# Five products of the input projection moved into the embedding and the experts' sum

## Chip, cores and metric

The kernel runs on one core of one Trainium2 chip. The metric is the device time of one execution in microseconds, the median of several runs. The engines are TensorE (PE; PEld is its weight load), VectorE (DVE), ScalarE (ACT), GpSimd (POOL) and SyncE (SP), which issues the DMAs.

## Reference, cut to what matters

The model is a stack of two mixed blocks (attention, a bidirectional recurrence, experts) and a third block of another kind. Only the start of each of the two mixed blocks is touched:

```python
h = _layer_norm(jnp.concatenate([meta, x], axis=1), emb_ln_g, emb_ln_b)   # the embedding
for li in range(DEPTH):                                                   # DEPTH = 2
    proj = h @ w_in[li]                                                   # the input product
    c_q, c_kv, k_pe, rw = _split(proj, [Q_LORA, KV_LORA, QK_ROPE, RWKV_COLS])
    y_att = _mla(c_q, c_kv, k_pe, cos, sin, ...)      # begins with rms norms of c_q and c_kv
    u = _centred_shift(rw, rwkv_mu_prev[li], rwkv_mu_next[li])
    ...
    ff = _hier_moe(...)                                                   # the experts and their sum
    h = _layer_norm(DN_ALPHA * h + ff, ln2_g[li], ln2_b[li])
```

There are 1040 tokens (16 meta tokens and 1024 others) of 1024 features; `w_in[li]` has 2368 columns.

## The kernel before, in words

**Stages.** The program is a sequence of stages, each written out per engine; between two of them every engine waits with `over` (L291) for all counts of the stage before. The stages here are the embedding (`embed_*`, L457 to L541), the input product with the small products of the attention's start (the front, `front_*`, L684 to L1110), and, after the experts of layer 0, their sum (`combine_*`, L2544 to L2630), which ends in the h of layer 1. The front of layer 1 follows it.

**Precision.** A float32 operand is split into two halves of the type fp32r: ScalarE copies it into `hi` (rounded), VectorE or GpSimd writes `lo` = x - hi. A product is three matmuls for each of the 8 slices of 128 features (`three`, L274): hi·hi, hi·lo, lo·hi.

**Tiles of tokens.** The embedding and the sum go over NT = 10 tiles of C = 104 tokens in rounds (`aged`, L451): in round r one step is done for tile r, the next for tile r-1, and so on. In the embedding the rounds are: statistics of tile r (L311 to L314); affine step of tile r-1 (L323, L326, L328); for tile r-2 the copy of its transposes into `hT.hi` (ScalarE, L524) and the subtraction into `hT.lo` (VectorE, L510). TensorE transposes a tile as soon as its affine step is done, in two halves of four 128-column pieces (L287), into six banks of PSUM in turn (eight in the sum), and waits for the subtraction of the tile that had the bank. The sum has one stage more: for tile r ScalarE scales the row of h (L2588), then VectorE adds two experts' rows times their gates (L2606), then the same norm, copy (L2583) and subtraction (L2615). SP stores each tile's h (L482, L2568) and loads the tile four further on into the same buffer once its transposes and its store are over (L470, L2552, L2554).

**The front.** `COLS` lists 19 blocks of 128 columns of w_in: two of the queries' low rank (n = 0, 1), one of keys and values (2), one of 64 columns for the rotated keys (3), and 15 of the recurrence. `GROUPS` cuts the tokens into groups of 416, 416 and 208, that is tiles 0 to 3, 4 to 7, 8 and 9. `front_order` (L577) yields (n, g) block by block, and with each the small products that stand behind it: `sum q` behind (2,1), which needs the squares of both query blocks over all tokens; `scale q` from (3,0) on, `turn pe` (the rotation of the keys, first user of the angles) from (4,0) on. The result of (n, g) goes into bank (3n + g) mod 6 of PSUM, small results into banks 6 and 7.

Weights have three buffers, `w[n % 3]`. SP loads block n+3 after product (n, 2) (`project_load`, L661); ScalarE makes `hi` (L867) during the block before, in the order of its list; `lo` is made by VectorE for even n and GpSimd for odd n (`half_lo`, L758, subtraction in L761). The products of the queries, of keys and values and of the rotated keys are copied out by ScalarE (L892). The angles of the rotation are worked out by VectorE in eight parts (`positions_dve`, L387) spread over the first eight steps of the front of layer 0; ScalarE makes sine and cosine behind (1,2) (`positions_act`, L426); SP stores and reloads them from (2,2) on (`positions_store`, L366).

In layer 0 the loads of blocks 0 to 2 are issued behind tiles 1 to 3 of the embedding, in layer 1 in the list at the start of the sum (`project_first`, L672). All their halves are made after the stage is over.

## Time and profile before

| | us |
|---|---|
| median of 3 runs | 5400.27 (5394.4 to 5401.44) |
| the profiled execution | 5393.46 |
| its span in the profile | 5391.6 |

| engine | busy us, share of the span |
|---|---|
| PE | 4819.5, 89% |
| PEld | 4154.7, 77% |
| DVE | 3312.1, 61% |
| ACT | 2134.1, 40% |
| POOL | 1304.3, 24% |

All times in rows are microseconds from the first instruction unless marked ns. "Idle before" is how long the engine had stood still, and the name behind the arrow is what ended it. The granted clock is a share of 2.4 GHz. SPq is SP's queue: the duration of a DMA row is that of its issue, not of the transfer.

### The profile page before, as it was taken

How to read it: one execution, taken by the hardware profiler on the slowest of the kernel's cores; microseconds unless marked ns; L12 is line 12 of the kernel's file. 1: busy time of each engine (PE TensorE's matmuls, PEld its weight loads, DVE VectorE, ACT ScalarE, POOL GpSimd, SP SyncE). 2: the span in 40 equal slices, each digit the busy share in tenths (PEclk: the TensorE clock that was granted, in tenths of full speed). 3: DMA queues.
4: the chain of work that ended last, by engine and by line, in shares of the span. 5: the costliest groups of instructions: out<-in, count | busy, mean ns of one | idle time of the engine just before them, and what ended most of it. 6: DMA issues, size and time to landing. Idle time of an engine off the chain costs nothing. (4 is left out here: it accounts for less than half of the span.)

```text
span 5391.6 us, 128874 instructions
## 1 busy us (share of the span) xinstructions
PE 4819.5 (89%) x56564; PEld 4154.7 (77%) x56564; DVE 3312.1 (61%) x5055; ACT 2134.1 (40%) x3885; POOL 1304.3 (24%) x940
## 2 busy tenths in 40 slices
PE   6989999998799957989999997799957988999999
PEld 5888888886588847878888886588845766788887
DVE  5435665557788864345665557788875465662662
ACT  2323333332188842433333332188843244232331
POOL 0012333332144510012333332144411100122221
PEclk9999999998799977989999998799978989999999
DMA  4420101003366653410101004366652101233332
GB/s 135 140 53 19 32 20 31 19 19 114 119 229 254 251 174 97 124 53 20 31 20 31 19 19 115 120 231 251 251 172 86 39 1 67 90 98 121 110 98 106
DMA packets 383087, 536.31 MB, mean 99 GB/s; under 512 B 136483, under 2 KB 306595, under 8 KB 354467
## 3 DMA queue, kind: packets, MB, share of 16 engines
q1 hardware_dynamic: 339714, 488.61, 28.3%
q0 software_dynamic: 41472, 34.21, 2.1%
q8 instruction: 450, 7.37, 0.6%
q10 hardware_dynamic: 1344, 5.24, 0.3%
q14 instruction: 107, 0.87, 0.1%
HBM read 573.01 MB, written 122.09 MB: 129 GB/s over the span
## 5 line engine op out<-in xcount | busy, mean ns | idle before, releaser
L280 PE MATMUL ps<-w_hi,xbT 128*128 128x512 f32 x1536 | 502.3, 398 | 18.0 <-DVE w L2437 18.0
L280 PE MATMUL ps<-hT,w_in 128*128 128x416 f32 (+1 forms) x2736 | 490.7, 338 | 9.0 <-DVE w_in L761 9.0
L280 PEld LDWEIGHTS ps<-hT,w_in 128*128 128x128 f32 x2736 | 457.3, 195 | 35.3 <-issue 29.3
L2437 DVE TENSOR_TENSOR w<-w,w_hi 128x2048 fp32r<-128x2048 f32 x192 | 429.9, 2278 | 2.2 <-ACT w_hi L2394 2.2
L1486 POOL TENSOR_TENSOR lm<-Ab,consts 116x416 f32<-116x416 f32 x240 | 254.8, 1069 | 592.0 <-PE ps L280 316.4
L2394 ACT ACTIVATE w_hi<-w 128x2048 fp32r<-128x2048 f32 x192 | 359.0, 1935 | 0.0
L280 PEld LDWEIGHTS ps<-w_hi,xbT 128*128 128x128 f32 x1536 | 289.6, 189 | 86.3 <-DVE w L2437 27.1
L280 PE MATMUL ps<-w,xbT 128*128 128x512 f32 x768 | 300.6, 391 | 0.0
L280 PE MATMUL ps<-v,pT 104*104 104x128 f32 (+1 forms) x2176 | 270.3, 280 | 28.2 <-issue 27.4
L2468 DVE TENSOR_TENSOR w<-w,w_hi 128x2048 fp32r<-128x2048 f32 x96 | 223.5, 2328 | 97.0 <-ACT w_hi L2430 97.0
L280 PEld LDWEIGHTS ps<-v,pT 104*104 104x104 f32 (+1 forms) x2176 | 248.8, 178 | 39.9 <-issue 32.4
L280 PE MATMUL ps<-w_hi,actT 128*128 128x512 f32 x768 | 253.5, 391 | 5.0 <-DVE actT L2463 5.0
L280 PE MATMUL ps<-x1T,w_gate 128*128 128x512 f32 x1056 | 249.5, 392 | 2.9 <-DVE x1T L3279 1.6
L280 PE MATMUL ps<-x1T,w_up 128*128 128x512 f32 x1056 | 246.5, 389 | 0.0
L280 PE MATMUL ps<-w_down,act 128*128 128x512 f32 x1056 | 241.6, 391 | 3.0 <-POOL w_down L3505 3.0
L280 PE MATMUL ps<-w_out,mixT 128*104 128x512 f32 x960 | 237.2, 403 | 2.3 <-DVE mixT L2046 2.3
L280 PEld LDWEIGHTS ps<-x1T,w_gate 128*128 128x128 f32 x1056 | 200.0, 190 | 45.5 <-issue 1.9
L280 PEld LDWEIGHTS ps<-w_down,act 128*128 128x128 f32 x1056 | 199.3, 189 | 45.0 <-POOL w_down L3505 3.4
L280 PEld LDWEIGHTS ps<-x1T,w_up 128*128 128x128 f32 x1056 | 198.2, 188 | 41.1
L3496 POOL TENSOR_TENSOR w_up<-w_up,w_up 128x1024 fp32r<-128x1024 f32 x44 | 116.1, 2640 | 459.1 <-ACT w_up L3418 459.1
L280 PE MATMUL ps<-T,lm 52*52 52x52 f32 x6400 | 192.2, 209 | 27.9 <-DVE TT L1430 19.6
L280 PEld LDWEIGHTS ps<-w_out,mixT 128*104 128x104 f32 x960 | 160.3, 169 | 71.7 <-DVE mixT L2046 11.2
(449 smaller groups left out, 11384.9 us busy)
## 6 DMA issues: line engine op xcount, KB each, us to landing
w<-in_moe_w_dram SPq DMA_DIRECT2D x192, 1024.0 KB, 10.0
w_gate<-in_w_gate_dram SPq DMA_DIRECT2D x44, 512.0 KB, 3.9
w_up<-in_w_up_dram SPq DMA_DIRECT2D x44, 512.0 KB, 3.9
w_down<-in_w_down_dram SPq DMA_DIRECT2D x44, 512.0 KB, 3.2
w_in<-in_w_in_dram SPq DMA_DIRECT2D x36, 512.0 KB, 4.3
ys<-t_ys SPq DMA_DIRECT2D x20, 832.0 KB
t_h<-x SPq DMA_DIRECT2D x30, 416.0 KB
w_out<-in_w_out_dram SPq DMA_DIRECT2D x24, 512.0 KB, 7.3
```

The costliest lines, as they stand in the source:

```text
L280: made = e.matmul(out, a, b, start=start, stop=stop)
L1486: e.tensor_tensor(m.LM[lv % 2][0:HP], m.ab[0:HP, :, 0, :], bc(m.lmask[0:HP, H * lv:H * lv + H].unsqueeze(1), [HP, 8, H]), ALU.mult).then_i ...
L2394: e.activation(w.hi, w.x, ACT.Copy).then_inc(*P.c("moe_act").tick(li, "w13", b, k))
L2437: e.tensor_tensor(w.lo, w.x, w.hf, ALU.subtract).then_inc(*P.c("moe_dve").tick(li, "w13", b, k))
L2468: e.tensor_tensor(w.lo, w.x, w.hf, ALU.subtract).then_inc(*dv.tick(li, "w2", b))
L3496: e.tensor_tensor(w.lo, w.x, w.hf, ALU.subtract).then_inc(*po.tick(0, c, "lo", f))
```

## The change

Five products of each layer, (0,0), (1,0), (2,0), (0,1) and (1,1), are issued by the embedding (layer 0) and by the experts' sum of layer 0 (for layer 1). TensorE goes through their slices with one generator for the five; behind the transposes of the embedding's tiles 0 to 9 stand 0, 0, 0, 0, 5, 5, 5, 5, 4, 16 of the 40 slices, behind those of tiles 4, 5, 6, 8, 9 of the sum 8 each. A product of block 0 waits for the subtraction of the last tile of its token group. Transposes use banks 6 and 7 for even tiles, 2 and 5 for odd ones, and wait for the subtraction two tiles back. The halves of blocks 0 to 2 are made inside the tiles: `hi` by ScalarE in rounds 2 to 4, `lo` by GpSimd for all three. ScalarE copies the five results out in late rounds. In layer 0 SP issues the three weight loads before the tiles instead of behind tiles 1 to 3. The front goes over the rest in the same order; the squares, the angles' parts, the sine and cosine, their store and the first halves of block 3 get other places in it.

```diff
@@ embed_sp
     positions_sp(e, P)
+    for n in range(3):
+        project_load(e, P, 0, n)
     for t in aged(NT, 3):
...
-        if t[2] in (1, 2, 3):
-            project_load(e, P, 0, t[2] - 1)
     project_first(e, P, 0)
+def turn_bank(P, i, half):
+    return P.ps[((6, 7), (2, 5))[i % 2][half]]
@@ embed_act
-    for t in aged(NT, 3):
+    for r, t in enumerate(aged(NT, 3)):
...
+        front_early_act(e, P, 0, r, (7, 9, 10, 11, 11))
@@ embed_pe
+    products = front_early_pe(e, P, 0, P.c("emb_dve"))
...
-            if i >= 3:
-                e.wait_ge(*P.c("emb_dve").at(0, i - 3, "lo", half))
-            psv = columns(P.ps[b], C)
+            if i >= 2:
+                e.wait_ge(*P.c("emb_dve").at(0, i - 2, "lo", half))
+            psv = columns(turn_bank(P, i, half), C)
...
+        for _ in islice(products, (0, 0, 0, 0, 5, 5, 5, 5, 4, 16)[i]):
+            pass
+EARLY = [(0, 0), (1, 0), (2, 0), (0, 1), (1, 1)]
+def late_order(li):
+    for n, g, here in front_order(li):
+        if (n, g) in EARLY:
+            assert not here
+        else:
+            yield n, g, here
@@ front_sp
-        if (n, g) == (2, 2) and li == 0:
+        if (n, g) == (3, 1) and li == 0:
             angles()
+def lo_taker(P, n):
+    return P.c("prj_pool" if n % 2 or n < 3 else "prj_dve")
+def front_early_pool(e, P, li):
+    for n in range(3):
+        half_lo(e, P, li, n, lo_taker(P, n))
+def front_hi(e, P, li, n):
+    w = P.frt.w[n % 3]
+    e.wait_ge(*P.d(f"prj_w{n % 3}_in").at(li, n))
+    e.activation(w.hi, w.x, ACT.Copy).then_inc(*P.c("prj_act").tick(li, "hi", n))
+def front_early_act(e, P, li, r, rounds_out):
+    if 2 <= r < 5:
+        front_hi(e, P, li, r - 2)
+    for at, (n, g) in zip(rounds_out, EARLY):
+        if at == r:
+            front_low_rank(e, P, li, n, g)
+def front_product(e, P, li, n, g):
+    w, (t0, tn) = P.frt.w[n % 3], GROUPS[g]
+    out = P.ps[(3 * n + g) % 6][:, 0:tn]
+    if g == 0:
+        e.wait_ge(*lo_taker(P, n).at(li, "lo", n))
+    if n >= 2:
+        e.wait_ge(*P.c("prj_act").at(li, "out", n - 2, g))
+    for k in range(8):
+        made = mms(e, three(out, w.at(k), P.hT.at(k, slice(t0, t0 + tn)), k == 0, k == 7))
+        if k == 7:
+            made.then_inc(*P.c("prj_pe").tick(li, n, g))
+        yield k
+def front_early_pe(e, P, li, rests):
+    for n, g in EARLY:
+        if n == 0:
+            e.wait_ge(*rests.at(0, 4 * g + 3, "lo", 1))
+        yield from front_product(e, P, li, n, g)
@@ front_act
-    hi(0)
-    for n, g, here in front_order(li):
+    for n, g, here in late_order(li):
-        if g == 0 and n + 1 < len(COLS):
-            hi(n + 1)
+        if ((n, g) == (2, 2) or n >= 3 and g == 0) and n + 1 < len(COLS):
+            front_hi(e, P, li, n + 1)
+        if (n, g) == (1, 2):
+            square(0, P.cq[:, 0, :], prj.at(li, "out", 0, 2))
+        if (n, g) == (2, 1):
+            square(1, P.cq[:, 1, :], prj.at(li, "out", 1, 2))
...
-        if (n, g) == (1, 2) and li == 0:
+        if (n, g) == (2, 2) and li == 0:
             positions_act(e, P)
@@ front_dve
-    half_lo(e, P, li, 0, prj)
+    angles = {(0, 2): (0, 1), (1, 2): (2, 3), (2, 1): (4, 5), (3, 0): (6, 7)}
...
-        if li == 0 and n < 3 and 3 * n + g < 8:
-            positions_dve(e, P, 3 * n + g)
+        for part in angles.get((n, g), ()) if li == 0 else ():
+            positions_dve(e, P, part)
@@ combine_act
+        if li == 0:
+            front_early_act(e, P, 1, r, (7, 8, 9, 11, 12))
@@ combine_pe
+    products = front_early_pe(e, P, 1, P.c("com_dve")) if li == 0 else None
...
+        if li == 0 and i in (4, 5, 6, 8, 9):
+            for _ in islice(products, 8):
+                pass
@@ gpsimd_program
+    front_early_pool(e, P, 0)
     for li in range(DEPTH):
...
+        if li == 0:
+            front_early_pool(e, P, 1)
```

## Rows read from the trace of the kernel before

**Rows 1.** Busy time by stretch: PE, PEld, DVE, ACT, POOL, clock, DMA, GB/s
```profile
340.00:360.00 20.00, 20.00 (x138) 19.55 (x135) 7.80 (x8) 5.02 (x7) 0.00 (x0) 1.00 0.00 1
```

**Rows 2.** Timeline of PE in the fronts: start, us, instructions, [idle before]
```profile
69.47 34.59 PE L280 MATMUL ps<-hT,w_in 128*128 128x416 f32 x192 [4.49 <-DVE w_in L761]
103.89 3.74 PE L280 MATMUL ps<-consts,squares 128*104 128x1 f32 x40
107.49 9.07 PE L280 MATMUL ps<-hT,w_in 128*128 128x208 f32 x48
...
2103.47 9.09 PE L280 MATMUL ps<-hT,w_in 128*128 128x208 f32 x48
```

**Rows 3.** Timeline of the embedding, layer 0: transposes and a tile's statistics
```profile
28.25 1.65 PE L287 MATMUL ps<-consts,x 104*128 104x104 f32 x8 [3.33 <-DVE x L328]
29.11 0.68 DVE L311 BATCH_NORM_STATS2 stat<-x 104x6 f32<-104x512 f32 x1
...
63.33 1.65 PE L287 MATMUL ps<-consts,x 104*128 104x104 f32 x8 [1.94 <-DVE x L328]
```

**Rows 4.** Timeline of the experts' sum, layer 0: the split of tile 7, the last transposes
```profile
2054.89 1.09 DVE L2615 TENSOR_TENSOR hT<-ps,hT 128x416 fp32r<-128x416 f32 x2 [0.77 <-ACT hT L2583]
...
2058.62 1.65 PE L287 MATMUL ps<-consts,h 104*128 104x104 f32 x8 [6.88 <-DVE h L328]
```

**Rows 5.** Timeline of ACT in the front of layer 0: copies of products
```profile
76.11 0.52 ACT L892 ACTIVATE cq<-ps 128x416 f32<-128x416 f32 x1 [7.10 <-PE ps L280]
80.64 0.52 ACT L892 ACTIVATE cq<-ps 128x416 f32<-128x416 f32 x1 [4.01 <-PE ps L280]
83.30 0.34 ACT L892 ACTIVATE cq<-ps 128x208 f32<-128x208 f32 x1 [2.15 <-PE ps L280]
...
112.07 0.35 ACT L892 ACTIVATE ckv<-ps 128x208 f32<-128x208 f32 x1 [4.13 <-PE ps L280]
```

**Rows 6.** Busy time by stretch, with the granted clock (columns as in rows 1)
```profile
70.00:75.00 5.00, 5.00 (x20) 4.82 (x19) 4.91 (x11) 0.00 (x0) 1.54 (x1) 1.00 0.68 204
104.00:112.00 8.00, 8.00 (x66) 8.00 (x65) 0.22 (x1) 2.07 (x3) 0.00 (x0) 0.79 0.01 2
...
2040.00:2060.00 20.00, 4.67 (x24) 3.99 (x24) 17.72 (x25) 4.36 (x10) 0.00 (x0) 0.50 0.23 65
...
2066.00:2068.00 2.00, 2.00 (x7) 1.91 (x6) 0.94 (x6) 0.00 (x0) 0.85 (x1) 0.50 1.02 227
...
2070.00:2072.00 2.00, 2.00 (x11) 1.98 (x11) 0.00 (x0) 0.00 (x0) 0.00 (x0) 0.92 1.05 364
```

**Rows 7.** View of the tile w_in: durations in ns (min/median/max), landing
```profile
L761 POOL TENSOR_TENSOR w_in<-w_in,w_in x18: 2363/2418/3166, 69.2 to 2346.8; 128x1024 fp32r<-128x1024 f32 x18
...
DMA to landing us min/median/max: 3.3/4.2/30.4
```

**Rows 8.** Timelines of POOL and of DVE in the front, near 194 us
```profile
194.71 2.42 POOL L761 TENSOR_TENSOR w_in<-w_in,w_in 128x1024 fp32r<-128x1024 f32 x1 [29.95 <-ACT w_in L867]
...
194.82 2.75 DVE L1078 TENSOR_TENSOR staged<-staged,cos 128x416 f32<-128x416 f32 x1
```

**Rows 9.** Timeline of DVE in the front of layer 0: first use of the angles
```profile
139.98 0.58 DVE L1076 TENSOR_TENSOR turned<-ps,sin 64x416 f32<-64x416 f32 x1 [0.41 <-PE ps L280]
```

**Rows 10.** Timeline of SP: a tile's load, weights in layer 1, the cosines
```profile
23.67 0.31 SPq L470 DMA_DIRECT2D x<-in_x_dram  x1
...
112.48 0.59 SPq L369 DMA_DIRECT2D t_cossin<-cos  x1
...
1962.61 27.57 SPq L669 DMA_DIRECT2D w_in<-in_w_in_dram  x3
```

**Rows 11.** Waits of DVE in the embedding, then in the sum: us, times, longest
```profile
DVE stat L311 <- DMA x<-in_x_dram: 1.4, 3, 0.7
...
DVE h L2606 <- ACT h L2588: 3.5, 1, 3.5
```

**Rows 12.** DMA issues up to 75 us: KB each, us to landing
```profile
rest<-in_positions_dram SPq DMA_DIRECT2D x1, 256.0 KB, 15.6
```

More of the change, by code:

```diff
@@ L2 @@
 from contextlib import ExitStack
-from itertools import groupby
+from itertools import groupby, islice
 import numpy as np
@@ L484, in embed_sp @@
             load(t[2] + 4)
-        if t[2] in (1, 2, 3):
-            project_load(e, P, 0, t[2] - 1)
     project_first(e, P, 0)
+def turn_bank(P, i, half):
+    return P.ps[((6, 7), (2, 5))[i % 2][half]]
 def embed_part(P, i, half):
-    return P.emb.hT.at(slice(4 * half, 4 * half + 4), slice(C * i, C * i + C)), columns(P.ps[2 * (i % 3) + half], C)
+    return P.emb.hT.at(slice(4 * half, 4 * half + 4), slice(C * i, C * i + C)), columns(turn_bank(P, i, half), C)
 def embed_dve(e, P):
@@ L761, in half_lo, with front_low_rank @@
     e.tensor_tensor(w.lo, w.x, w.hf, ALU.subtract).then_inc(*count.tick(li, "lo", n))
+def lo_taker(P, n):
[7 more added lines that the diff above has]
+    e.activation(w.hi, w.x, ACT.Copy).then_inc(*P.c("prj_act").tick(li, "hi", n))
+def front_low_rank(e, P, li, n, g):
+    kind, j, _, wd = COLS[n]
+    t0, tn = GROUPS[g]
+    into = P.cq[:, j, :] if kind == "q" else P.ckv if kind == "kv" else P.kpe
+    e.wait_ge(*P.c("prj_pe").at(li, n, g))
+    e.activation(into[0:wd, t0:t0 + tn], P.ps[(3 * n + g) % 6][0:wd, 0:tn], ACT.Copy).then_inc(
+        *P.c("prj_act").tick(li, "out", n, g))
+def front_early_act(e, P, li, r, rounds_out):
[21 more added lines that the diff above has]
+        yield from front_product(e, P, li, n, g)
 def front_pool(e, P, li):
-    for n in range(1, len(COLS), 2):
-        half_lo(e, P, li, n, P.c("prj_pool"))
+    for n in range(3, len(COLS), 2):
+        half_lo(e, P, li, n, lo_taker(P, n))
 def small_bank(number):
@@ L793, in spread @@
                  True) for k in range(tn // C) for to, x in parts]
-    for n, g, here in front_order(li):
-        w, (t0, tn) = m.w[n % 3], GROUPS[g]
-        if g == 0:
-            e.wait_ge(*P.c("prj_pool" if n % 2 else "prj_dve").at(li, "lo", n))
-        if n >= 2:
-            e.wait_ge(*P.c("prj_act").at(li, "out", n - 2, g))
-        out = P.ps[(3 * n + g) % 6][:, 0:tn]
-        mms(e, [y for k in range(8) for y in three(out, w.at(k), P.hT.at(k, slice(t0, t0 + tn)), k == 0, k == 7)]
-            ).then_inc(*prj.tick(li, n, g))
+    for n, g, here in late_order(li):
+        for _ in front_product(e, P, li, n, g):
+            pass
         for number, name in here:
@@ L872, in square @@
         e.activation(m.sums[k], src, ACT.Square).then_inc(*ac.tick(li, "square", k))
-    hi(0)
     earlier = []
-    for n, g, here in front_order(li):
+    for n, g, here in late_order(li):
         kind, j, _, wd = COLS[n]
         t0, tn = GROUPS[g]
-        if g == 0 and n + 1 < len(COLS):
-            hi(n + 1)
-        src = P.ps[(3 * n + g) % 6]
-        if kind == "u":
+        if ((n, g) == (2, 2) or n >= 3 and g == 0) and n + 1 < len(COLS):
[4 more added lines that the diff above has]
+            square(1, P.cq[:, 1, :], prj.at(li, "out", 1, 2))
+        if kind != "u":
+            front_low_rank(e, P, li, n, g)
+        else:
+            src = P.ps[(3 * n + g) % 6]
             dst, src = m.pt[n % 2][:, 1 + t0:1 + t0 + tn], src[:, 0:tn]
@@ L887, in front_act @@
                 e.wait_ge(*dv.at(li, "right", 1))
-        else:
-            into = P.cq[:, j, :] if kind == "q" else P.ckv if kind == "kv" else P.kpe
-            dst, src = into[0:wd, t0:t0 + tn], src[0:wd, 0:tn]
-        e.wait_ge(*P.c("prj_pe").at(li, n, g))
-        e.activation(dst, src, ACT.Copy).then_inc(*prj.tick(li, "out", n, g))
+            e.wait_ge(*P.c("prj_pe").at(li, n, g))
+            e.activation(dst, src, ACT.Copy).then_inc(*prj.tick(li, "out", n, g))
         if kind == "u" and g == 2:
@@ L1001, in front_dve @@
     earlier, turned = [], None
[L1002 to L1003 removed]
+    angles = {(0, 2): (0, 1), (1, 2): (2, 3), (2, 1): (4, 5), (3, 0): (6, 7)}
+    for n, g, here in late_order(li):
+        if n >= 3 and g == 0 and n + 1 < len(COLS) and (n + 1) % 2 == 0:
             half_lo(e, P, li, n + 1, prj)
[L1005 removed]
+        if n >= 3 and g < 2:
             shifted(n - 1, g)
[L1007 to L1008 removed]
+        for part in angles.get((n, g), ()) if li == 0 else ():
+            positions_dve(e, P, part)
         if (n, g) == (3, 0):
@@ L2540, in combine_part @@
     s = (P.xT2 if li else P.hT).at(slice(4 * half, 4 * half + 4), slice(c0, c0 + C - skip))
-    return s, columns(P.ps[2 * (i % 4) + half], C)[:, :, skip:C]
+    return s, columns(turn_bank(P, i, half), C)[:, :, skip:C]
 def combine_sp(e, P, li):
@@ L2574, in combine_act @@
     m, ac = P.com, P.c("com_act")
-    for t in aged(NT, 4):
+    for r, t in enumerate(aged(NT, 4)):
         if t[1] is not None:
```

22 lines of the change are left out of this document (5 added, 17 removed).

## The prediction

> **What bounds the kernel now.** The page puts TensorE first, so I went to its rows by stage. Inside the input product it never rests: it is busy in all of 340 to 360 us [rows 1], and from 69.47 us its rows follow each other without a gap [rows 2]. Any matmul taken out there is time taken off, as long as nothing else arrives late. In the two stages ahead of it, the embedding and the experts' sum of layer 0 (called the sum below), VectorE sets the pace and TensorE waits: in a tile's round it transposes for 1.65 us and sits idle for 3.33 us, in the sum 6.88 us [rows 3, 4]. So the change moves matmuls from a stage that TensorE bounds into two that it doesn't. I write (n,g) for the product of block n with token group g.
>
> **Price of a product.** The copies of (0,0), (0,1) and (0,2) start at 76.11, 80.64 and 83.30 us [rows 5]: 4.53 us for 24 matmuls of 416 columns, 2.66 us for 24 of 208. The five early ones are all of 416: 22.65 us a layer.
>
> **Layer 0, the path.** Before: the last transposes end at 63.33 + 1.65 = 64.98 us [rows 3]; then TensorE idles 4.5 us until block 0 is split; product (0,0) to (2,1) run to 103.89, the 40 matmuls of the sum of squares to 107.49, (2,2) to 111.9 (its copy starts at 112.07) [rows 2, 5]. That is 46.9 us from the last transpose to the start of (3,0). After: (0,0), (1,0) and (2,0) are over by then. Their 24 steps of three matmuls go 5, 5, 5, 5, 4 behind tiles 4 to 8; 15 matmuls take 15/24 of 4.53 = 2.83 us, and with the transposes' 1.65 us this is 4.5 us in a round of some 5.0, so the next transposes aren't late by more than 0.3 us. Behind tile 9 come (0,1) and (1,1), 9.06 us, of which only the former 4.5 us of idling is cover; then (0,2) and (1,2) 5.32, (2,1) 4.53, sum of squares 3.60, (2,2) 4.4. Sum 26.9, with the 0.3 us 27.2 us. **Gain 46.9 - 27.2 = 19.7 us.** It is less than 22.65 + 4.5, since two of the five "early" products stand behind the last tile in the path, and more than three products since the split of block 0 and the slow start go.
>
> **The clock.** (2,2) costs 4.4 us and not 2.66 us since it runs after the one-column matmuls: 104 to 112 us has a granted clock of 0.79, a mix of 1.2 and 2.4 GHz [rows 6]. The change keeps that order, so I keep the price. The sum runs at 0.50 (1.2 GHz). The front of layer 1 begins after 4.5 us of idling like that of layer 0, at 2064.8 us, and still has 0.50 in 2066 to 2068 and 0.92 in 2070 to 2072 [rows 6]. I take 5.5 us at the slow level: 15.8 matmuls of 416/1.2 = 347 ns, then 8.2 of 189 ns, 7.05 us for a first product. In layer 0 the stretch 70 to 75 us reads 1.00 but holds only 20 matmuls, 250 ns each [rows 6]; I take it as the same rise. The first steps behind tile 4 then take 5.2 us and push the transposes of tile 5 by 1.4 us; ScalarE copies those only a round later, so nothing waits. The Trainium skill, "TensorE: Matmul & The Clock Gate" (Part 1), says that the slow level is the resting state and that sustained work releases it; the rows of the sum agree.
>
> **Layer 1, the path.** Before: the transposes end at 2058.62 + 1.65 = 2060.27 us [rows 4], and (3,0) starts 4.4 us after the row of 2103.47 us [rows 2], at 2107.9: 47.6 us. After: (0,0) waits behind the transposes of tile 4 for the split of tile 3, in the next round; (0,0), (1,0) and (2,0) then fit into rounds that leave TensorE 6.88 us each. (0,1), behind the transposes of tile 8, waits for the split of tile 7: 2054.89 + 1.09 = 2056.0 us [rows 4], with TensorE at the slow level again. It takes 7.05 us, to 2063.0, so the transposes of tile 9 end at 2064.65 instead of 2060.27. From there (1,1) 4.53, (0,2) and (1,2) 5.32, (2,1) 4.53, 3.60, 4.4: (3,0) starts at 2087.0 instead of 2107.9. **Gain 20.9 us.**
>
> **What the change adds.** Three splits a layer go to GpSimd, 2.42 us each [rows 7], and three first halves to ScalarE, inside the tiles. ScalarE is mostly idle there. GpSimd is another matter. At 194.82 us a VectorE multiply with two SBUF inputs lasts 2.75 us because a split on GpSimd began 0.11 us ahead of it [rows 8]; free, an operation of that width takes 0.58 us [rows 9]. VectorE is the bound of the tiles' stages. In the embedding GpSimd's split falls due while VectorE is in its last affine step, and behind it stand the transposes' subtraction (one input in PSUM) and the statistics (one input), 1.08 + 1.5 us, which hide 2.4 us: 0. In the sum, the two products with the gates stand right behind the affine step, both with SBUF inputs. Block 0's load was issued at 1962.6 and the longest landing is 30.4 us [rows 7, 10]: it lands about 1992.5, and ScalarE, which waits for it in order, gives the square root and the copy of tile 0 some 2.7 us late. That delay and GpSimd's splits of blocks 0 and 1 (2.3 us) come ahead of a wait of VectorE of 3.5 us for tile 4's row [rows 11], which swallows most of it: left 1.6 us, then the split of block 2, 2.3 us. I take 3.9 us; bounds 0 and 3 x 2.4 = 7.2 us.
>
> **Loads of layer 0.** The three weight loads (1.5 MB) now stand ahead of the first store of h. The queue had drained by 4.5 + 15.6 = 20.1 us [rows 12]; now it drains about 5 us later. Tile 4's load waits for that store: issued at 23.67 before [rows 10], some 4 us later now, so it lands near 32 us and the statistics of 29.11 us [rows 3] start 2.8 us late. In return the three waits of VectorE on later tiles, 1.4 us [rows 11], go, since no weights compete there. Net loss 1.4 us; bounds: a gain of 1.4 and a loss of 5.
>
> **Moved steps that I cost at nothing.** Block 3's load is issued after (0,2), at 77 us, behind SP's list of small loads; it lands 4.2 us later at the median [rows 7], its first half stands in ScalarE's queue behind the square root at 88 us, and the split ends at 91.8 us, just ahead of 92.2. The cover is (2,2) at the slow level; were (2,2) at 2.66 us, (3,0) would wait 1.4 us. In layer 1 SP's list comes 4.7 us later and block 3 is still ready before (3,0). The angles move behind (2,2): between the store of the cosines at 112.48 us [rows 10] and their first use at 139.98 us [rows 9] lie 27.5 us; now the store comes 8 us after the start of (3,0), at 100, and the use 28.1 us after it, at 120. The 20 us left cover a store, a reload and their issue at 4.2 us a landing. VectorE reaches the scaling of the queries later, and the next small product waits 0.7 us in layer 0: counted. The banks: transposes keep four instead of six or eight, but wait for a subtraction two tiles back, long done. The low-rank copies fall into idle time of ScalarE.
>
> **Sum.** Layer 0: 19.7 - 1.4 - 0.7 = 17.6. Layer 1: 20.9 - 3.9 = 17.0. Together 34.6 us. The profiled execution took 5393.46 us (span 5391.6) and would take 5358.9; it stands 6.8 us below the median of the runs, 5400.27, and from that the forecast is **5365.7 us**.
>
> **Rivals.** *(A) No losses.* The tiles' load comes in time, GpSimd finds gaps: 19.7 + 1.4 - 0.7 + 20.9 = 41.3 us, 5359 us. For it: a split that meets VectorE at a step with one input costs nothing. Chance 0.2.
> *(B) Each of the six splits holds VectorE in full*, 14.4 us instead of 3.9: gain 24.1, 5376 us. It needs VectorE at a two-input instruction each time. The Trainium skill, "SBUF — State Buffer" (Who interferes with whom), states this rule: whoever issues first gets the shared pair for the whole instruction, the other blocks; the rows at 194.8 us agree, and by it the time depends on what stands next in VectorE's queue. Chance 0.13.
> *(C) TensorE stays at 1.2 GHz through the tiles.* The 15 matmuls take 5.2 us, a round of the embedding 6.9 instead of 5.0: 9.5 us over five rounds, (0,1) and (1,1) 7.7 us more, in the sum some 5 us. Gain 12, 5388 us. Against it: at 2064.8 us the clock rose within 6 us of dense matmuls. Were the loads late as well, no change is left. Chance 0.05.
> *(D) Slower: the tiles starve.* Load of tile i waits for the store of tile i-4, and this queues behind weights. If each of the six later tiles came late, VectorE would pay each time; it decides from 7.6 us a tile (45.4 us lost against 34.6 gained): 5411 us. Against it: the queue is empty of weights after the first, and those waits were 0.7 us at most. Chance 0.02.
> That it doesn't do what it says is half true in layer 0 (two of five are behind the last tile) and in the sum already.
>
> **Chances.** Forecast 0.6. The range 5352 to 5381 us takes in (A), (B), the bounds above and a median that moves by a few us. A measurement here can tell 0.2%, 10.8 us, from no change: faster by more than that 0.94, within it 0.04, slower 0.02.
>
> **What would show it.** Right: matmuls of w_in from some 41 us on and from 2022 us on; (3,0) starting 92 to 95 us and near 2091 us; no idle time of TensorE there above 2 us. GpSimd's first three splits beside VectorE's two-input steps of some 3.5 us in the sum. Wrong: TensorE idle ahead of (3,0), rounds of the embedding above 5.5 us from tile 5 on, or a front stage that gives the time back after (3,0).

## The result and the profile after

The changed kernel takes 5363.57 us at the median of four runs (5362.61 to 5367.15), the kernel before 5399.22 us in four runs (5394.4 to 5401.44) made beside them: a ratio of 0.9933, 95% interval 0.9917 to 0.9949, that is 35.7 us less. The forecast was 5365.7 us. The profiled execution has a span of 5362.6 us, 29.0 us less than the 5391.6 of before; where the other 6 us of the profile stayed is told below.

The timeline of TensorE in the embedding and in the front of layer 0, changed kernel (columns: start, us, then engine, line, instruction, count, idle time before and what ended it):

```profile
40.92 1.65 PE L287 MATMUL ps<-consts,x 104*128 104x104 f32 x8 [3.33 <-DVE x L328]
42.27 4.04 PE L280 MATMUL ps<-hT,w_in 128*128 128x416 f32 x15
...
46.80 3.07 PE L280 MATMUL ps<-hT,w_in 128*128 128x416 f32 x15
50.88 0.93 PE L287 MATMUL ps<-consts,x 104*128 104x104 f32 x8 [1.01 <-DVE x L328]
...
64.43 0.93 PE L287 MATMUL ps<-consts,x 104*128 104x104 f32 x8 [0.37 <-DVE x L328]
65.14 19.19 PE L280 MATMUL ps<-hT,w_in 128*128 128x416 f32 x120
84.16 3.74 PE L280 MATMUL ps<-consts,squares 128*104 128x1 f32 x40
87.77 9.07 PE L280 MATMUL ps<-hT,w_in 128*128 128x208 f32 x48
96.67 1.93 PE L280 MATMUL ps<-consts,rms 104*128 104x104 f32 x16
```

The first rows answer to the embedding's of before [rows 3]: behind the transposes of tiles 4 to 7 now stand 15 matmuls each, and the idle time of 3.33 us ahead of the next tile's has shrunk to 1.2 at most. After the last tile TensorE doesn't stop; before it stood still for 4.49 us [rows 2]. The last row serves as a mark from here on: the first "spread" of the norm's factors, 16 matmuls right behind (3,0). Before it stood here:

```profile
116.40 1.93 PE L280 MATMUL ps<-consts,rms 104*128 104x104 f32 x16
```

So layer 0 is 19.73 us ahead at this mark. Some of that is scatter at the very start: the statistics of tile 1 begin at 15.15 us before and at 15.81 here, and counted from them it is 20.4 us. The same view for layer 1, from the sum to the same mark:

```profile
2007.56 6.11 PE L280 MATMUL ps<-hT,w_in 128*128 128x416 f32 x24 [4.29 <-DVE hT L2681]
...
2014.16 4.77 PE L280 MATMUL ps<-hT,w_in 128*128 128x416 f32 x24
...
2041.65 6.12 PE L280 MATMUL ps<-hT,w_in 128*128 128x416 f32 x24 [4.29 <-DVE hT L2681]
2047.61 0.88 PE L287 MATMUL ps<-consts,h 104*128 104x104 f32 x8
2048.26 14.66 PE L280 MATMUL ps<-hT,w_in 128*128 128x416 f32 x96
2062.76 4.90 PE L280 MATMUL ps<-consts,squares 128*104 128x1 f32 x40
```

The spread of layer 1 starts at 2076.89 us, 35.51 us ahead of the 2112.40 of before. The sum itself began 19.07 us earlier; SP's first load of it, before and after, is the second mark:

```profile
1957.98 0.33 SPq L2552 DMA_DIRECT2D ys<-t_ys  x1
```

```profile
1938.91 0.33 SPq L2616 DMA_DIRECT2D ys<-t_ys  x1
```

Layer 1 adds 16.44 us. What VectorE did in the sum's first rounds (timeline of VectorE, changed kernel; L323 and L328 are the affine steps, L2672 the products with the gates, L2681 the subtraction out of PSUM), and GpSimd beside it:

```profile
1976.18 1.09 DVE L2681 TENSOR_TENSOR hT<-ps,hT 128x416 fp32r<-128x416 f32 x2 [3.54 <-ACT hT L2647]
1977.18 1.98 DVE L323 SCALAR_TENSOR_TENSOR h<-h,stat,gain 104x1024 f32<-104x1024 f32 x1
...
1979.27 3.17 DVE L328 SCALAR_TENSOR_TENSOR h<-h,stat,bias 104x1024 f32<-104x1024 f32 x1
1982.37 2.59 DVE L2672 SCALAR_TENSOR_TENSOR h<-ys,gates,h 104x1024 f32<-104x1024 f32 x2
...
1990.88 4.69 DVE L2672 SCALAR_TENSOR_TENSOR h<-ys,gates,h 104x1024 f32<-104x1024 f32 x2
```

```profile
1975.73 2.35 POOL L781 TENSOR_TENSOR w_in<-w_in,w_in 128x1024 fp32r<-128x1024 f32 x1 [38.22 <-ACT w_in L796]
1978.52 2.84 POOL L781 TENSOR_TENSOR w_in<-w_in,w_in 128x1024 fp32r<-128x1024 f32 x1 [0.44 <-ACT w_in L796]
1990.28 2.89 POOL L781 TENSOR_TENSOR w_in<-w_in,w_in 128x1024 fp32r<-128x1024 f32 x1 [8.92 <-ACT w_in L796]
```

The affine steps lasted 1.27 and 1.28 us before, and take 1.98 and 3.17 where a split of GpSimd (the subtraction that makes `lo`) runs; the products with the gates of tile 4 lasted 2.61 and take 4.69: 0.71 + 1.89 + 2.08 us.

### The profile page after: what moved, and what is told of

It reads as the page before. It is cut to its first block and busy times, and to the rows that moved or that the text cites. A ratio compares the mean times of both kernels' runs of the same rounds, so it can differ in the third digit from the quotient of the medians.

```text
span 5362.6 us, 128881 instructions
## 1 busy us (share of the span) xinstructions
PE 4821.6 (90%) x56564; PEld 4156.3 (78%) x56564; DVE 3307.6 (62%) x5051; ACT 2133.3 (40%) x3885; POOL 1314.0 (25%) x944
## 5 line engine op out<-in xcount | busy, mean ns | idle before, releaser
L280 PEld LDWEIGHTS ps<-w_hi,xbT 128*128 128x128 f32 x1536 | 291.1, 190 | 87.0 <-DVE w L2501 27.2
```

Source lines behind the costliest of these rows:

```text
L280: made = e.matmul(out, a, b, start=start, stop=stop)
```

## The experiments

Each kernel was timed in rounds with the kernel before, and the ratio is against the median of the kernel before in the same rounds (5397.59 to 5402.88 us; 5399.22 is that of the first measurement). Since one median moves by a few us, I also read the marks in each profile: the first spread of layer 0, the start of the sum, the first spread of layer 1 and the span. What stands behind the third mark is the same program in all of them; the last column is the span less that mark. Where two numbers stand for "changed", the second is the second measurement (e5). The marks scatter too: the statistics of tile 1 start at 14.5 to 16.0 us, with every placing of the loads alike, and VectorE's first affine step of the sum, which waits for the row of the affine parameters, starts 18.3 to 20.2 us after the sum.

| kernel | median us | ratio (95%) | spread, layer 0 | sum starts | spread, layer 1 | sum to spread | span | rest |
|---|---|---|---|---|---|---|---|---|
| before | 5399.22 | | 116.40 | 1957.98 | 2112.40 | 154.42 | 5391.6 | 3279.2 |
| changed | 5363.57 / 5359.80 | 0.9933 / 0.9928 | 96.67 / 96.29 | 1938.91 / 1937.61 | 2076.89 / 2075.46 | 137.98 / 137.85 | 5362.6 / 5358.0 | 3285.7 / 3282.5 |
| e1 layer 0 alone | 5375.25 | 0.9959 (0.9946 to 0.9973) | 98.44 | 1937.22 | 2091.80 | 154.58 | 5377.6 | 3285.8 |
| e2 layer 1 alone | 5373.82 | 0.9954 (0.9940 to 0.9968) | 117.52 | 1961.67 | 2100.20 | 138.53 | 5375.8 | 3275.6 |
| e3 none inside | 5397.38 | 0.9998 (0.9989 to 1.0008) | 112.78 | 1954.68 | 2106.64 | 151.96 | 5392.2 | 3285.6 |
| e4 splits held | 5358.27 | 0.9923 (0.9909 to 0.9936) | 95.91 | 1933.92 | 2067.47 | 133.55 | 5357.4 | 3289.9 |
| e6 loads behind tiles | 5363.95 | 0.9942 (0.9929 to 0.9954) | 100.38 | 1943.17 | 2080.69 | 137.52 | 5359.9 | 3279.2 |
| e7 more slices | 5361.77 | 0.9931 (0.9918 to 0.9945) | 95.65 | 1938.62 | 2076.45 | 137.83 | 5358.6 | 3282.2 |
| e8 sums spread | 5361.88 | 0.9936 (0.9924 to 0.9949) | 98.09 | 1939.80 | 2077.83 | 138.03 | 5360.0 | 3282.2 |
| e9 loads, splits timed | 5362.69 | 0.9930 (0.9916 to 0.9943) | 98.28 | 1937.15 | 2068.25 | 131.10 | 5353.6 | 3285.3 |
| e10 all together | 5354.35 | 0.9918 (0.9904 to 0.9931) | 95.98 | 1934.70 | 2068.62 | 133.92 | 5347.8 | 3279.2 |
| e11 held, more slices | 5358.84 | 0.9920 (0.9907 to 0.9934) | 93.33 | 1934.77 | 2068.66 | 133.89 | 5358.2 | 3289.5 |
| e12 and loads behind tiles | 5358.40 | 0.9925 (0.9911 to 0.9938) | 93.00 | 1935.88 | 2068.79 | 132.91 | 5354.9 | 3286.1 |

### One layer alone

e1 keeps the sum, the front of layer 1 and GpSimd's program of before; e2 the embedding and the front of layer 0:

```diff
+def front_pe(e, P, li):                       # likewise sp, act, dve, pool
+    return (front_pe_whole if li == 1 else front_pe_rest)(e, P, li)   # e2: li == 0
-        if li == 0:                           # e1; combine_* as before
-            front_early_pool(e, P, 1)
-    front_early_pool(e, P, 0)                 # e2; embed_* as before
```

> The change in the embedding and the front of layer 0 alone; the sum of layer 0 and the front of layer 1 as before. Theory (the two halves are independent and nearly equal, 17.6 and 17.0 us by the prediction): gain 17.6 us against before, a ratio of 0.9967, and (3,0) of layer 0 starts near 92.2 us, (3,0) of layer 1 at 2107.9 - 17.6 = 2090 us. Rival (one half carries nearly all of the 35.7 us measured, the other gives its part back later): ratio at 0.993 or at 1.000.

> The change in the sum of layer 0 and the front of layer 1 alone; the embedding and the front of layer 0 as before. Theory: gain 17.0 us, ratio 0.9969; (3,0) of layer 1 starts near 2091 us; GpSimd's splits again hold VectorE in the sum (multiplies of 1.3 us at 2 to 3 us). Rival: as for the other half.

By the marks layer 0 alone is 17.96 us ahead at its spread, and its layer 1 takes the 154.6 us of before. Layer 1 alone takes 138.5 us from the start of the sum to the spread, 15.9 less than before, with the same stretched steps of VectorE. So in the marks the halves are independent and nearly equal, as the theory has it. The medians say 22.6 and 24.0 us. The interval of e1 takes in the expected ratio of 0.9967; that of e2 ends at 0.9968, just short of 0.9969. Both can't be right beside the 35.7 of the whole; the marks add up to 33.9. e2's profile also has the shortest rest of all, 3275.6 us, with the same instructions there: medians of five runs are too coarse to split a gain of this size.

### No product inside

```diff
-        for _ in islice(products, (0, 0, 0, 0, 5, 5, 5, 5, 4, 16)[i]):
+        for _ in islice(products, (0, 0, 0, 0, 0, 0, 0, 0, 0, 40)[i]):
...
-        if li == 0 and i in (4, 5, 6, 8, 9):
-            for _ in islice(products, 8):
+        if li == 0 and i == 9:
+            for _ in products:
```

ScalarE's copies of the five results move to the last round (round 11 for all five in the embedding, round 12 in the sum).

> Everything of the change but the place of the five products: in both layers all 40 slices stand behind the transposes of the last tile, and ScalarE copies the results out in its last round. Banks, halves and loads stay as changed. Theory (the gain is TensorE's idle time filled, the rest is small): layer 0 loses 24 slices x 0.566 us = 13.6 us of its gain; in layer 1 three products (13.6 us) and the one behind tile 8 (6.1 us at the slow clock, of which the transposes' own wait gave back some 4.4) come back, some 16 to 18 us. Together 30 to 32 us lost of 35.7: 4 to 6 us faster than before, ratio 0.999. Rival (the halves made early and the filled wait of 4.5 us ahead of the front are the main gain): ratio 0.996 or lower.

The median is 0.5 us below that of before, no difference; the marks give 3.62 us in layer 0 and 2.46 from the start of the sum to the spread, and at the last mark the kernel is 5.8 us ahead, in the range expected, of which its rest gave 6.4 back. TensorE, behind the last transposes of each layer:

```profile
65.11 33.71 PE L280 MATMUL ps<-hT,w_in 128*128 128x416 f32 x192
...
2059.47 34.82 PE L280 MATMUL ps<-hT,w_in 128*128 128x416 f32 x192
```

The idle time of 4.5 us between stage and front has gone here too, in both layers. That part of the change is real but small; the place of the matmuls carries the gain.

### GpSimd's splits in the sum

```diff
 def front_early_pool(e, P, li):
     for n in range(3):
+        if li:
+            e.wait_ge(*P.c("com_dve").at(0, 3 + n, "y", 1))
         half_lo(e, P, li, n, lo_taker(P, n))
```

> The changed kernel, but in the sum GpSimd starts each of its three splits only when VectorE has finished the products with the gates of tiles 3, 4 and 5, that is while VectorE stands at the statistics, a wait and the subtraction out of PSUM. Theory (the splits hold VectorE at instructions with two SBUF inputs: 0.7 + 1.9 + 2.1 us in the changed kernel's sum; the late weights' 2.8 us are swallowed by the wait for tile 4): the multiplies are back at 1.3 and 2.6 us, tile 4's statistics start 3.9 us earlier against the start of the sum, and the kernel is 3.9 us faster than the changed one (5359.7 us). Rival (the late weights alone set the time of tile 4): multiplies faster, tile 4's statistics where they were, same time as the changed kernel. Second rival (the splits hit other steps instead): three stretched instructions elsewhere, same time or slower.

The same rounds of VectorE, and GpSimd beside them:

```profile
1970.71 1.28 DVE L323 SCALAR_TENSOR_TENSOR h<-h,stat,gain 104x1024 f32<-104x1024 f32 x1
...
1972.09 1.28 DVE L328 SCALAR_TENSOR_TENSOR h<-h,stat,bias 104x1024 f32<-104x1024 f32 x1
...
1982.68 2.61 DVE L2674 SCALAR_TENSOR_TENSOR h<-ys,gates,h 104x1024 f32<-104x1024 f32 x2 [0.79 <-ACT h L2654]
```

```profile
1976.16 2.34 POOL L781 TENSOR_TENSOR w_in<-w_in,w_in 128x1024 fp32r<-128x1024 f32 x1 [43.62 <-DVE h L2674]
```

All three stretched steps are back at 1.28 and 2.6 us, and GpSimd's own are shorter (2.34 instead of 2.84 and 2.89). Tile 4's statistics start 51.41 us after the sum's first load, 56.70 in the changed kernel: 5.3 us earlier, where 3.9 were expected (0.9 us of the difference is the row of the affine parameters, which landed that much earlier against the sum's start); from the sum to the spread it is 4.43 us less. The cause of VectorE's loss is shown: the same instructions, the same loads, only the moment of the splits moved. The same holds for the four kernels below that hold these splits (e9 to e12): none of their affine steps and products with gates in the sum lasts over 1.31 us. The wait for tile 4 of 3.5 us [rows 11] is now one of 0.79: the late weights, which hold ScalarE back by 2.1 us here, took most of the rest, and tile 4's row came 0.6 us earlier. The median is 5.3 us below the first measurement of the changed kernel and 1.5 below the second; the medians alone would not carry the verdict.

### The changed kernel once more

> The changed kernel once more, unaltered, to see what one profile and another of the same program differ by. Theory (stretches with the same instructions differ between profiles by single steps of 1.6 to 2.9 us, where TensorE comes back from an idle stretch at 1.2 instead of 2.4 GHz, whatever the kernel): median within 3 us of 5363.6, the front of layer 0 ends its sum of squares and (2,2) within 2 us of the first profile, and the stretch behind the first small products of layer 1, 3285.8 us before, differs by several us. Rival (the 6.5 us that the profile gave back there belong to the change): that stretch is again within 1 us of 3285.8.

The rest behind the spread of layer 1 took 3282.5 us, 3.2 less than in the first profile of the same program, and in the other profiles of this unchanged stretch 3275.6 to 3289.9. The rival falls. The median, 5359.80 us, is 3.8 us from the first one's 5363.57, where at most 3 was expected. One such step: the experts of layer 1, where TensorE comes back after 2.7 us of idling. First the profile of the changed kernel above, then this one (PE's timeline, then busy time by stretch, in the columns of [rows 1]):

```profile
3489.03 0.79 PE L280 MATMUL ps<-w_hi,xbT 128*128 128x512 f32 x1 [2.72 <-DVE w L2501]
...
3490.00:3492.00 2.00, 2.00 (x6) 1.56 (x5) 2.00 (x2) 2.00 (x2) 1.85 (x1) 0.50 0.03 0
```

```profile
3481.16 0.50 PE L280 MATMUL ps<-w_hi,xbT 128*128 128x512 f32 x1 [2.73 <-DVE w L2501]
...
3482.00:3484.00 2.00, 2.00 (x10) 1.65 (x9) 2.00 (x2) 2.00 (x2) 1.73 (x1) 1.00 0.06 8
```

The same instructions after the same idle time, once at 1.2 GHz (granted clock 0.50, 6 matmuls in 2 us), once at 2.4 (10 matmuls). The profile of before had 1.00 here as well. This step costs 2.9 us by the time TensorE is back at 2.4 GHz; with one of 2.6 us in the output product ahead of it that is 5.5 of the 6.5 us that the first profile of the changed kernel gave back behind the mark; smaller ones of both signs stand beside them. What decides between the two levels these profiles don't show.

### The loads of layer 0

```diff
-    for n in range(3):
-        project_load(e, P, 0, n)
     for t in aged(NT, 3):
...
+        if t[2] in (1, 2, 3):
+            project_load(e, P, 0, t[2] - 1)
@@ front_early_act: halves of layer 0 in rounds 4 to 6
-    if 2 <= r < 5:
-        front_hi(e, P, li, r - 2)
+    at = 2 if li else 4
+    if at <= r < at + 3:
+        front_hi(e, P, li, r - at)
```

> The changed kernel with layer 0's weight loads back behind tiles 1 to 3 and the first halves of layer 0 made in rounds 4 to 6 instead of 2 to 4. Theory (the three loads ahead of the first store make tile 4's row 2.7 us late, and take away three small waits of 1.4 us): statistics of tile 4 at 29.1 instead of 31.8 us, waits of 0.4 to 0.7 us ahead of three later tiles, (3,0) of layer 0 1.4 us earlier, at 90.8 us. Rival (the delay of tile 4 is the queue's, full of the positions' small packets, and not the weights'): tile 4 as late as in the changed kernel, and the later waits on top: 1.4 us slower.

Tile 4 in the changed kernel, SP and VectorE, and then tile 4 here:

```profile
5.76 15.33 SPq L689 DMA_DIRECT2D w_in<-in_w_in_dram  x2
...
27.78 0.31 SPq L470 DMA_DIRECT2D x<-in_x_dram  x1
...
31.82 0.69 DVE L311 BATCH_NORM_STATS2 stat<-x 104x6 f32<-104x512 f32 x1 [1.69 <-DMA x<-in_x_dram]
```

```profile
28.88 0.69 DVE L311 BATCH_NORM_STATS2 stat<-x 104x6 f32<-104x512 f32 x1
```

Tile 4 is in time again, 2.9 us earlier, of which 0.9 is the earlier start of this profile (2.0 us counted from the statistics of tile 1): the first half of the theory holds. But the kernel is 3.7 us behind at the spread instead of 1.4 ahead. The splits now fall elsewhere:

```profile
37.51 3.17 DVE L328 SCALAR_TENSOR_TENSOR x<-x,stat,bias 104x1024 f32<-104x1024 f32 x1
...
43.04 3.05 DVE L323 SCALAR_TENSOR_TENSOR x<-x,stat,gain 104x1024 f32<-104x1024 f32 x1
...
51.17 3.18 DVE L328 SCALAR_TENSOR_TENSOR x<-x,stat,bias 104x1024 f32<-104x1024 f32 x1
```

```profile
37.22 2.38 POOL L781 TENSOR_TENSOR w_in<-w_in,w_in 128x1024 fp32r<-128x1024 f32 x1 [36.77 <-ACT w_in L796]
```

Three affine steps of 1.23 to 1.28 us last 3.05 to 3.18: 5.6 us lost. In the changed kernel the same three splits cost 0.27 us in all (one affine step of 1.50). This is the prediction's rival B, made by moving the loads. Nothing in my expectation allowed for it.

### Loads and splits timed; all together

e9 issues the three loads right behind tile 4's, and GpSimd waits for an affine step's end (`embed_norm(P, 3 + n).done(e)`, in layer 1 as in e4):

```diff
         if t[2] is not None and t[2] + 4 < NT:
             load(t[2] + 4)
+            if t[2] == 0:
+                for n in range(3):
+                    project_load(e, P, 0, n)
```

> The changed kernel with the sum's splits held as before (behind the products with the gates of tiles 3 to 5), and in layer 0 the three weight loads issued together right behind tile 4's load, the first halves made in rounds 4 to 6, and GpSimd's splits held until VectorE has finished the affine step of tiles 3, 4 and 5, so that they run beside the subtraction out of PSUM and the statistics. Theory (in the kernel with the loads behind the tiles, tile 4 came 2.9 us earlier, and three splits that met two-input steps took 1.9 us each from VectorE; without these only the first remains): statistics of tile 4 at 29.0 us, no affine step above 1.5 us, the last transposes of the embedding 2 to 3 us earlier than the changed kernel's 64.43 us; with the sum's 4 to 5 us the kernel is 6 to 8 us faster than the changed one. Rival (tile 5's row now queues behind the weights and comes late instead): statistics of tile 5 2 to 3 us late, gain in layer 0 nil, 4 to 5 us in all.

No affine step of the embedding is above 1.29 us. But the rival has it in layer 0: tile 5's row is late now, by 3.3 us (timeline of SP, then of VectorE):

```profile
24.27 5.63 SPq L690 DMA_DIRECT2D w_in<-in_w_in_dram  x3
...
38.41 0.69 DVE L311 BATCH_NORM_STATS2 stat<-x 104x6 f32<-104x512 f32 x1 [3.33 <-DMA x<-in_x_dram]
```

Against the changed kernel the spread of layer 0 is 1.6 us later (2.0 counted from the statistics of tile 1); the sum is where the gain is, 131.1 us to its spread instead of 138.0. Not all of these 6.9 us belong to the edit: e4 and e10 hold the same splits and have 133.6 and 133.9, since there the affine parameters land 1.0 and 1.3 us later and the stretch behind the start of the sum of squares takes 14.1 us instead of 12.5. Of the 6 to 8 us expected the third mark shows 7.2 to 8.6; the median, 0.9 us below the first measurement of the changed kernel and 2.9 above the second, shows none of it.

### More slices behind the tiles

```diff
-        for _ in islice(products, (0, 0, 0, 0, 5, 5, 5, 5, 4, 16)[i]):
+        for _ in islice(products, (0, 0, 0, 0, 6, 6, 6, 6, 5, 11)[i]):
```

> The changed kernel with 6, 6, 6, 6, 5, 11 slices behind tiles 4 to 9 of the embedding instead of 5, 5, 5, 5, 4, 16. TensorE idles 1.0, 1.2, 1.2 and 0.4 us ahead of the transposes of tiles 6 to 9; a slice takes 0.57 to 0.61 us. Theory (five more slices fit into these 3.8 us): the last transposes end at 65.4 us as now or up to 0.5 us later, 5 x 0.57 = 2.8 us less stands behind them: (3,0) of layer 0 2.3 to 2.8 us earlier. Rival (ScalarE copies (0,0) out only in round 7, (2,0) now waits for it behind tile 6, and the next transposes with it): no gain, the rounds longer by the wait.

```profile
65.31 16.37 PE L280 MATMUL ps<-hT,w_in 128*128 128x416 f32 x105
81.51 3.96 PE L280 MATMUL ps<-consts,squares 128*104 128x1 f32 x40
85.33 10.48 PE L280 MATMUL ps<-hT,w_in 128*128 128x208 f32 x48
```

The sum of squares starts 2.65 us earlier (81.51 instead of 84.16), as the theory wants, and the last transposes stand 0.3 us later against those of tile 4. Then the matmuls behind it take 10.48 instead of 9.07 us, and the spread is only 1.0 us earlier. In e11, which has the same slices, they take 9.07, and the spread stands at 93.33: the 2.65 us were there, and what the clock takes behind them varies from profile to profile.

### The norm's sums spread

```diff
-        for _ in front_product(e, P, li, n, g):
-            pass
+        for k in front_product(e, P, li, n, g):
+            if between:
+                made = mms(e, between[20 * k // 8:20 * (k + 1) // 8])
...
+            if kind == "sum q":
+                between, between_tick = mats, pe.tick(li, "small", number)
+                continue
@@ front_act: block 3's first half behind the copy of (2,1)
```

> The changed kernel, with the one-column matmuls of the queries' norm no longer in one row of 3.7 to 4.9 us behind (2,1) but two or three behind each slice of (2,2), in both layers; the first half of block 3 is made behind the copy of (2,1), so that its split doesn't become late. Theory (the row of one-column matmuls lets TensorE fall to 1.2 GHz, and (2,2) and the start of (3,0) pay): no stretch of 0.50 behind it; from the end of (2,1) to the first spread of the norm 3.6 + 2.66 + 4.53 = 10.8 us in both layers instead of 12.5 (layer 0) and 14.1 us (layer 1): 5 us faster in all. Rival (the clock falls for the same matmuls wherever they stand, or for the 208-column product): the same 12.5 and 14.1 us. Second rival (block 3's split becomes the wait ahead of (3,0)): an idle time of TensorE of 1 to 2 us there.

```profile
88.00:90.00 2.00, 2.00 (x20) 2.00 (x21) 0.00 (x0) 0.00 (x0) 0.23 (x1) 0.92 0.00 0
90.00:92.00 2.00, 2.00 (x10) 1.97 (x10) 0.22 (x1) 0.89 (x3) 0.00 (x0) 0.50 0.24 45
92.00:94.00 2.00, 2.00 (x7) 1.90 (x7) 0.00 (x0) 1.99 (x3) 0.00 (x0) 0.50 0.76 225
```

My theory falls. The mixed stretch runs at 2.4 GHz almost to its end at 90.9 us, and then the clock is granted at 0.50 just the same, now under the dense matmuls of (3,0), which take 7.34 us for 24. From the end of (2,1) to the spread it is 13.7 us in layer 0 and 14.2 in layer 1 (12.5 and 14.1 in the changed kernel): nothing gained, as the first rival has it. In layer 1 the second rival shows as well, 0.75 us of idling ahead of (3,0) for the split of block 3.

### The versions put together

> The same, and 6, 6, 6, 6, 5, 11 slices behind the embedding's tiles. Theory (2.65 us fewer in the path ahead of the norm's sums, as measured with this edit alone): 8 to 10 us faster than the changed kernel, near 5353 us. Rival (TensorE's clock falls further behind the one-column matmuls, as it did with this edit alone, 10.5 instead of 9.1 us for the 48 matmuls behind them): no more than 1 us better than the kernel without this edit.

> The changed kernel with the two edits that helped alone: the sum's splits held behind the products with the gates of tiles 3 to 5, and 6, 6, 6, 6, 5, 11 slices behind the embedding's tiles; the loads of layer 0 where the change has them. Theory (the loads behind tile 4's row made tile 5's 3.3 us late, those ahead of the tiles make tile 4's some 2 us late, so this place is the better by 1.5 us): last transposes of the embedding by 64.8 us, sum of squares of layer 0 at 81.5 us, 4.4 to 5.3 us less from the start of the sum to the small products of layer 1; near 5353 us. Rival (the placing of the loads makes no difference): 5354 to 5358 us, as the version with all edits and the one with the held splits alone.

e12 is e11 with the loads of e6 and, in layer 0, the splits held behind the affine steps of tiles 4 to 6:

```diff
+        else:
+            embed_norm(P, 4 + n).done(e)
         half_lo(e, P, li, n, lo_taker(P, n))
```

> The version with held splits in the sum and 6, 6, 6, 6, 5, 11 slices, with layer 0's weight loads one behind each of tiles 1 to 3, their first halves in rounds 4 to 6, and GpSimd's splits of layer 0 held until VectorE has finished the affine steps of tiles 4, 5 and 6. With this placing of the loads tile 4 came 2.9 us earlier, but 5.6 us went to stretched affine steps and 0.8 us to a wait for tile 5's row. Theory (the stretched steps are all that spoils this placing): no affine step above 1.3 us, the last transposes 2 us earlier than in the version without the placing (63.96 us), the first spread of layer 0 near 91.3 instead of 93.3 us. Rival (the later splits now hold TensorE, which waits for block 0's behind tile 4 and for the next two blocks' behind tiles 5 and 6, and ScalarE's wait for late weights delays the square roots): idle times of TensorE ahead of the first products, last transposes no earlier than 63.96 us, spread at 93 us or later.

No affine step is above 1.29 us, so the hold has taken away all 5.6 us of e6, and tile 4 is in time: the first part of the theory holds. But tiles 5, 6 and 7 wait 0.55, 0.50 and 0.86 us for their rows, and TensorE 0.88 us for block 0's split, as the rival has it:

```profile
40.76 4.99 PE L280 MATMUL ps<-hT,w_in 128*128 128x416 f32 x18 [0.88 <-POOL w_in L781]
...
63.63 0.88 PE L287 MATMUL ps<-consts,x 104*128 104x104 f32 x8
```

```profile
45.61 0.69 DVE L311 BATCH_NORM_STATS2 stat<-x 104x6 f32<-104x512 f32 x1 [0.86 <-DMA x<-in_x_dram]
```

The last transposes start 0.33 us earlier than in e11, and so does the spread (93.00), where 2 us were expected. And this profile simply starts earlier: its tile 1 has its statistics at 14.53 us, that of e11 at 15.39. Counted from there the last transposes start after 49.1 us in e12, 48.6 in e11 and in the changed kernel, and 50.6 and 50.8 in e9 and e10. So with the splits out of VectorE's way, loads behind the tiles (three rows a little late) gain nothing over loads ahead of them (one row late), and loads issued in one go behind tile 4's are the worst by 2 us.

e10 has the lowest median of the study, 5354.35 us (ratio 0.9918, 0.9904 to 0.9931), close to the 5353 expected of it; its interval overlaps that of the changed kernel. But the marks don't bear its theory out. At the spread of layer 0 it is 2.3 us ahead of e9, the kernel without the extra slices, as expected; at the spread of layer 1 it stands at 2068.62 us and e9 at 2068.25, which is what the rival said. Its low span comes from the rest, 3279.2 us against e9's 3285.3, with the same instructions.

e11 should have come near 5353 us too and has 5358.84, beyond even its rival's 5358, although its marks in layer 0 are nearly all there (last transposes at 63.96 us, sum of squares at 80.81, spread 2.65 us ahead of e10's). Up to the spread of layer 1 e10 and e11 are level, 2068.6 us, 6.8 to 8.3 us ahead of the changed kernel's two profiles; behind it e11's rest is 3289.5. So holding the splits and giving the tiles more slices beats the changed kernel by some 7 us in the traces, and the kernel before by some 44, but the medians can't rank e4, e10, e11 and e12.

## Why the prediction was right

**Layer 0, the path.** From the end of the last transposes to (3,0) I had 27.2 us against 46.9. Measured from 65.36 us to the spread, which is (3,0) later: 31.3 us, forecast 27.2 + 4.53 = 31.7, before 51.4. (3,0) itself starts at 92.09 us, inside the 92 to 95 given as a sign. The rounds went as worked out; the first 15 matmuls took 4.04 us in one profile and 5.20 in the other (forecast 5.2), and no later tile was held up by it in either. The granted clock explains the two values, but its column doesn't show it: the clock's record in the trace begins, with 1.00, at 44.4 us in the first profile, at 46.5 in e5 and only at 73.5 in the kernel before, and ahead of its first entry the views print 1.00 as well. The 1.00 of [rows 6] at 70 to 75 us is such a case, and reading it as the rise to 2.4 GHz was right.

**Layer 0, the loads.** SP's issue of the weights lasted 15.33 us, so tile 4's load went out at 27.78 instead of 23.67 us (forecast some 4 us), and its statistics started 2.7 us late (forecast 2.8). That agreement is partly luck, since 0.7 us of it stood there already at the statistics of tile 1, whose start scatters that much with either placing of the loads; counted from them, tile 4 is 2.05 us late here and 1.9 in e5, so the term was some 0.8 us too large. The later waits went. Yet the last transposes end at 65.36 us against 64.98, 0.4 us late and not 1.4: the three waits and the rounds gave back 1.6, and those transposes take 0.93 us instead of 1.65, with TensorE at 2.4 GHz by then (the record of 1.00 from 44.4 us on; before, it begins behind them). That I had not counted. So at the spread layer 0 had gained 19.7 us in the first profile and 20.1 in e5, against the 18.3 that the sum has up to there.

**The wait for "scale q", 0.7 us.** This step was wrong. The sum has TensorE wait there for VectorE's scaling, which comes later in the new order; in fact TensorE goes through the small products at 103 us without idling. In its place the first profile has the clock: the 48 matmuls behind the next 20 one-column matmuls take 9.08 us, and 7.45 in e5 and in the profile of before. The granted clock of 104 to 108 us is 0.73 in the first profile and 1.00 in e5. That is the 1.6 us by which the gain of 19.73 at the spread becomes 18.1; in e5 it stays at 20.1. So the 17.6 us of layer 0 were some 2.5 us too few, and in the first profile the clock hid most of that.

```profile
105.18 9.08 PE L280 MATMUL ps<-hT,w_in 128*128 128x208 f32 x48
```

```profile
124.91 7.45 PE L280 MATMUL ps<-hT,w_in 128*128 128x208 f32 x48
```

**Layer 1.** Forecast 20.9 - 3.9 = 17.0, measured 16.4 to the spread, 15.9 in e2. The 3.9 us, step by step at tile 4's statistics: ScalarE late for the weights 2.8 us (forecast 2.7); GpSimd's first two splits 2.6 (2.3); the wait for tile 4 swallowed 3.5 (3.5); the third split 2.1 (2.3). Sum 4.0. A further 0.8 us came from the affine parameters, whose row landed 0.8 us later against the sum's start; that stood in no step, and by the spread of this row over the profiles (18.3 to 20.2 us) it is scatter. e4 shows the part of GpSimd by taking it away. The clock made two errors that nearly cancel. From start to start (0,1) took 6.0 us and not 7.05, and the transposes behind it 0.65 and not 1.65; the sum of squares took 4.8 and not 3.6, and the two products behind it 9.4 and not 8.9. The load of block 0 was said to land at 1992.5 us; with the 30.4 us named it would be 1993.0, but that load itself took 29.8, and 1992.4 is right. The sign given for layer 1, (3,0) near 2091 us, left out what layer 0 gains: it fits e2, which has layer 1 alone, while in the changed kernel (3,0) starts at 2072.35 us.

**Moved steps.** Block 3's split ended at 91.69 us (forecast 91.8), ahead of (3,0) at 92.09, and nothing waited for the angles. The cover was as thin as said: in e8 the same split made (3,0) of layer 1 wait 0.75 us.

**Rivals.** (A) needed both losses to be nil; the sum's were 4. (B), every split in full, was not what this placing does: 0.27 us of three splits in the embedding, 4.7 in the sum. But e6 shows the mechanism at 1.9 us a split. The Trainium skill, "SBUF — State Buffer" (Who interferes with whom), says that a VectorE instruction with two SBUF inputs contends with GpSimd's reads, and that whoever issues first holds the shared pair. The stretched rows and, in e4, their absence beside statistics and a subtraction out of PSUM agree with it. (C) is refuted: 15 matmuls take 3.07 us from the second round on, and the sum has a granted clock of 1.00 in 2015 to 2020 us. (D) would have needed 7.6 us a tile; one row was 2.7 us late.

**The median.** The profile of before stood 6.8 us below its median, and I added that to the forecast. The changed kernel's profiled execution, 5364.45 us, stands 0.9 us above its median; steps of the clock, as the one shown above, are most of what the two profiles differ by behind the last mark. The forecast of the profiled span, 34.6 us less, missed the 29.0 measured mainly by what was no part of the change; in e5 it was 33.6. The median was met within 2.1 us the first time and within 5.9 the second, so a good part of the closeness is luck; what holds is the gain up to the last mark, 35.5 us in one profile and 36.9 in the other, with layer 0 some 2 us above its forecast and layer 1 half a us below.

## What to carry to other kernels

Work taken from a stage that TensorE bounds into the idle time of a stage that VectorE bounds was worth its full price here, less what its helpers cost the stage that receives it; count those by the instruction they land beside, not by their length. A split of 2.4 us on GpSimd was free beside the statistics and the subtraction out of PSUM, and cost VectorE up to 2.1 us beside a step with two SBUF inputs, so tie it to a point in VectorE's order. Loads moved elsewhere move the splits too (e6). And compare stages between marks in two traces: here the same 3280 us of program varied by 14 us between profiles.

## What I had not expected of the hardware

TensorE after the same idle time of 2.7 us ran at 1.2 GHz in one profile and at 2.4 in another of the same program. The clock also fell behind 40 one-column matmuls while TensorE had no idle time at all (granted 0.69 in 88 to 90 us and 0.50 in 90 to 92), and spreading these among dense matmuls only moved the fall by a microsecond or two (e8). An issue on SP can be long: most last 0.3 to 0.4 us, but two weight loads right behind the positions' load in the embedding took 15.3 us, and three in the sum 28.9 (27.6 before [rows 10]); in e9, later in the embedding, three took 5.6. That the transfers already in the queue hold the issue is my reading; no run tests it.

```profile
1943.33 28.90 SPq L689 DMA_DIRECT2D w_in<-in_w_in_dram  x3
```
